# Two layers of a gated delta rule beside a linear recurrence: its gates computed per token in columns instead of per head in rows

## What is computed

```python
def l2norm(x):
    return x * lax.rsqrt(jnp.sum(x * x, axis=-1, keepdims=True) + L2_EPS)
...
    q = l2norm(qkv[..., :512].reshape(B, S, 4, 128))          # after conv and silu
    k = l2norm(qkv[..., 512:1024].reshape(B, S, 4, 128))
    beta = jax.nn.sigmoid(gb)
    g = -jnp.exp(gdn_a_log) * jax.nn.softplus(ga + gdn_dt_bias)   # (token, head)
...
    gc = jnp.cumsum(g, within a chunk of 64)
    decay = jnp.exp(jnp.where(tril, gc[..., :, None] - gc[..., None, :], -jnp.inf))
    a_mat = jnp.where(strict, (k * beta) @ k.T * decay, 0.0) + I
    u, w = solve(a_mat, [v * beta, k * beta * exp(gc)])
    # scan over chunks uses q * exp(gc), k * exp(gc_last - gc), exp(gc_last)
```

## Time and profile before

| | us |
|---|---|
| median of 3 runs (lowest, highest) | 2260.6 (2257.97, 2263.47) |
| the profiled execution, its own time | 2264.03 |
| its span | 2261.9 |
| PE busy in it | 2154.1 |
| DVE, ACT, POOL busy in it | 1321.4, 903.5, 622.4 |

### The profile page before, as it was taken

How to read it: one execution, slowest core, us unless ns; L and a number is a source line. 1 busy time by engine, 2 the same in 40 slices (tenths; PEclk the granted TensorE clock), 3 DMA queues, 4 the chain that set the end, 5 groups by cost and what they waited for, 6 DMA issues and landing times.

```text
span 2261.9 us, 25487 instructions
## 1 busy us (share of the span) xinstructions
PE 2154.1 (95%) x9704; PEld 1601.9 (71%) x9704; DVE 1321.4 (58%) x2006; ACT 903.5 (40%) x1410; POOL 622.4 (28%) x282
## 2 busy tenths in 40 slices
PE   8999999998999999999998999999999899999997
PEld 6777864766777864677766866777777578667776
DVE  4787845456788845457588724434165987244341
ACT  4432254433432354433563233445245543244441
POOL 2232420333233320333332300124433322002252
PEclk9999999997999999999998999999999899999999
DMA  6223321422323321323221012113232200111132
...
DMA packets 48047, 180.24 MB, mean 80 GB/s; under 512 B 5554, under 2 KB 6450, under 8 KB 46520
## 3 DMA queue, kind: packets, MB, share of 16 engines
...
...
q10 hardware_dynamic: 128, 0.13, 0.0%
...
## 4 chain that ended last, share of the span: by engine, by line
PE 72%; DVE 23%; ACT 2%; issue 2%; DMA 0%; DVEq 0%; ACTq 0%
PE bank L575 12%; PE bank L584 11%; PE bank L589 11%; PE bank L692 5%; PE bank L846 4%; PE bank L704 2%; PE bank L1058 2%; PE bank L1038 2%; PE bank L859 1%; PE bank L711 1%; PE bank L775 1%; PE bank L620 1%; PE bank L789 1%; DVE arena L1819 1%; DVE arena L1823 1%
## 5 line engine op out<-in xcount | busy, mean ns | idle before, releaser
L2344 POOL TENSOR_TENSOR w_lo<-wraw,w_hi 128x1024 fp32r<-128x1024 f32 (+1 forms) x222 | 548.6, 2473 | 1469.1 <-ACT w_hi L1126 1469.1
L1126 ACT ACTIVATE w_hi<-wraw 128x1024 fp32r<-128x1024 f32 (+1 forms) x222 | 233.7, 1053 | 679.7 <-PE bank L589 438.3
L575 PE MATMUL bank<-h_hi,w_hi 128*128 128x512 f32 (+1 forms) x1584 | 416.8, 406 | 8.7 <-ACT w_hi L1126 7.5
L584 PE MATMUL bank<-h_lo,w_hi 128*128 128x512 f32 (+1 forms) x1584 | 395.2, 391 | 0.2
L589 PE MATMUL bank<-h_hi,w_lo 128*128 128x512 f32 x1552 | 383.5, 389 | 0.0
L575 PEld LDWEIGHTS bank<-h_hi,w_hi 128*128 128x128 f32 (+1 forms) x1584 | 298.0, 191 | 107.9 <-issue 45.2
L584 PEld LDWEIGHTS bank<-h_lo,w_hi 128*128 128x128 f32 (+1 forms) x1584 | 298.4, 188 | 66.7 <-DVE h_lo L1658 1.7
L589 PEld LDWEIGHTS bank<-h_hi,w_lo 128*128 128x128 f32 x1552 | 290.1, 187 | 61.8
L692 PE MATMUL bank<-arena,wdir 128*128 128x512 f32 x256 | 114.3, 598 | 0.0
L846 PE MATMUL bank<-arena,wdir 128*128 128x512 f32 x208 | 97.8, 606 | 0.1
L2255 DVE TENSOR_TENSOR bank<-bank,con 128x128 f32<-128x128 f32 x64 | 19.2, 299 | 133.2 <-PE bank L1044 132.1
...
## 6 DMA issues: line engine op xcount, KB each, us to landing
...
```

What stands on the lines that cost most here:

```text
L575: mm(ps[0:wd, 0:S], hi[:, k, :].bitcast(F32R), h_hi[:, k, :].bitcast(F32R), start=k == 0 and not begun, stop=False)
L584: ins = mm(ps[0:wd, 0:S], hi[:, k, :].bitcast(F32R), h_lo[:, k, :].bitcast(F32R), start=False, stop=bool(parts) and k == KT - 1)
L1126: a(w_hi[:, n % 2, 0:f].bitcast(F32R), wraw[:, n % 2, 0:f], ACT.Copy).then_inc(hi_done, 1)
L2344: nc.gpsimd.tensor_tensor(w_lo[:, n % 2, 0:f].bitcast(F32R), wraw[:, n % 2, 0:f], w_hi[:, n % 2, 0:f], ALU.subtract).then_inc(lo_done, 1)
```

## The change

The gates are computed with tokens in the partitions: 128 partitions by 16 columns (4 blocks of 128 tokens, 4 heads) in place of 4 partitions by 512 tokens.

- `gba`'s 36 rows are copied as they are and turned by 4 transposes (`gT`). Sigmoid, the added bias, absolute value, exponential and `log1p_of` work on 128 x 16.
- The scan within a chunk becomes a product with the 0/1 matrix `incl`, and the chunk's total a product with a new matrix `chunk_` (`gC`, 2 matmuls). `constants` sends 128 more columns for it.
- Beta and cumulative decay are turned back as eight rows at once (`gR`, 4 transposes), split in two float32r parts by ACT (`rows_hi`) and DVE (`rows_lo`). `sel` shrinks to one column a row, read with stride 0.
- The 8 sums of squares become 32 products of a 128 x 128 block with one column of ones (`l2`), rooted and inverted as 128 x 32 and turned back by 4 transposes (`lR`). `l2sq` has room for all 8 squares.
- The 16 transposes `gN` and their copy go, since the columns are there already.
- The orders of PE, ACT and DVE are written anew around these.

The diff, cut to its core:

```diff
+        jobs += [("gc", l, j) for j in range(4, 8)] + [("gba", l), ("gc", l, 8), ("gc", l, 9), ("gT", l)]
+        jobs += [("gc", l, 10), ("gc", l, 11), ("lz", l, 0), ("gC", l), ("lz", l, 1), ("gR", l), ("lz", l, 2), ("lz", l, 3)]
+        jobs += [("gB", l, h, 1) for h in range(H)] + [("l2", l), ("mq", l, 0), ("lR", l), ("mq", l, 1)]
+        jobs += [("lb", l, j) for j in range(8)] + [("mq", l, 2)]
+        jobs += [("gB", l, h, 0) for h in range(H)] + [("mkv", l, j) for j in range(3)]
...
-                    return mm(ps[:, 0:S], sel[:, h * P:(h + 1) * P].bitcast(F32R), rows[:, n, :].bitcast(F32R),
+                    return mm(ps[:, 0:S], sel[:, h:h + 1].bitcast(F32R).broadcast_to([PAIR, P]), rows[:, n, :].bitcast(F32R),
...
+                ps = take("gT", l)
+                pe.wait_ge(*after("g_raw", l))
+                for tt in range(NT):
+                    ins = nc.tensor.transpose(ps[:, tt * GATES:(tt + 1) * GATES], graw[:, tt * P:(tt + 1) * P], ident[0:GATES, 0:GATES])
+                ins.then_inc(filled("gT", l), 1)
+                tile("gc", 10)
+                tile("gc", 11)
+                tile("lz", 0)
+                ps = take("gC", l)
+                pe.wait_ge(*after("g_col", l))
+                mm(ps[:, 0:16], incl, g_acc, start=True, stop=True)
+                mm(ps[:, 16:32], chunk_, g_acc, start=True, stop=True).then_inc(filled("gC", l), 1)
+                tile("lz", 1)
+
+                def to_rows(job, src):
+
+                    ps = take(*job)
+                    for tt in range(NT):
+                        ins = nc.tensor.transpose(ps[0:2 * H, tt * P:(tt + 1) * P], src(tt), ident)
+                    ins.then_inc(filled(*job), 1)
+
+                pe.wait_ge(*after("decays", l))
+                to_rows(("gR", l), lambda tt: gN[:, 16 * tt:16 * tt + 2 * H])
+                tile("lz", 2)
+                tile("lz", 3)
                 if l == 0:
                     pe.wait_ge(*after("sel"))
+                for h in range(H):
+                    ps = take("gB", l, h, 1)
+                    pe.wait_ge(*after("gc_rows", l))
+                    broadcast(ps, H + h, 1).then_inc(filled("gB", l, h, 1), 1)
+                ps = take("l2", l)
+                for n in range(8):
+                    pe.wait_ge(*after("l2_sq", l, n))
+                    for tt in range(NT):
+                        ins = mm(ps[:, 8 * tt + n:8 * tt + n + 1], l2sq[:, n, tt * P:(tt + 1) * P], ones[:, 0:1],
+                                 start=n == 0 and tt == 0, stop=n == 7 and tt == NT - 1)
+                ins.then_inc(filled("l2", l), 1)
+                tile("mq", 0)
+                pe.wait_ge(*after("l2_inv", l))
+                to_rows(("lR", l), lambda tt: l2col[:, 8 * tt:8 * tt + 8])
+                tile("mq", 1)
...
-                link(a(gates[:, 0, :], bank("gba", l)[0:H, 0:S], ACT.Sigmoid))
-                a(tmp4[:, 1, :], bank("gba", l)[32:32 + H, 0:S], ACT.Copy).then_inc(release("gba", l), 1)
-                for j in range(8, 12):
-                    conv_mid(j)
+                a(graw, bank("gba", l)[0:GATES, 0:S], ACT.Copy).then_inc(release("gba", l), 1)
+                act.wait_ge(*read("gba", l))
+                act.sem_inc(up("g_raw", l), 1)
+                conv_mid(8)
+                conv_mid(9)
+                act.wait_ge(*full("gT", l))
+                a(gcol4[:, :, 0, :], bank("gT", l)[:, 0:NT * GATES].rearrange("p (t r) -> p t r", t=NT)[:, :, 0:H],
+                  ACT.Sigmoid).then_inc(up("g_sig", l), 1)
+                conv_mid(10)
+                conv_mid(11)
 
                 act.wait_ge(*after("ga_dt", l))
-                link(a(tmp4[:, 1, :], tmp4[:, 0, :], ACT.Abs))
-                link(a(tmp4[:, 1, :], tmp4[:, 1, :], ACT.Exp, scale=-1.0))
-                a(small[0:H, 44:45], heads4[:, l, 0:1], ACT.Exp).then_inc(up("ga_y", l), 1)
+                link(a(g_y, g_x, ACT.Abs))
+                link(a(g_y, g_y, ACT.Exp, scale=-1.0))
+                a(g_scale, heads[:, l, 0, :], ACT.Exp).then_inc(up("ga_y", l), 1)
...
-                    if j == 3:
-                        act.wait_ge(*after("gc_sb", l, 3))
-                        for q in range(4):
+                    if j in (3, 7):
+                        act.wait_ge(*after("gc_sb", l, j))
+                        for q in range(j - 3, j + 1):
                             a(l2sq[:, q, :], gqkv(q), ACT.Square).then_inc(up("l2_sq", l, q), 1)
                     if j in (2, 9):
                         await_split("lz", l, 1 if j == 2 else 2)
+                    if j == 5:
+                        rows_hi(("gR", l), 1, 0)
                     if j in (5, 8):
                         silu_z(j // 4 - 1)
                 await_split("lz", l, 3)
-                act.wait_ge(*full("l2", l, 0))
-                act.wait_ge(*after("gc_sb", l, 7))
-                for j in range(4, 8):
-                    a(l2sq[:, j % 4, :], gqkv(j), ACT.Square).then_inc(up("l2_sq", l, j), 1)
-                row_root(("l2", l, 0), row_q, 1)
                 silu_z(2)
-                keep(("mq", l, 0), cq[:, 0, :])
                 silu_z(3)
-                row_root(("l2", l, 1), row_k, 1)
                 act.wait_ge(*after("decays", l))
-                a(tmp4[:, 0, :], gates[:, 1, :], ACT.Exp).then_inc(up("exp_gc", l), 1)
-                a(gates[:, 3, :], tmp4[:, 1, :], ACT.Exp).then_inc(up("exp_rest", l), 1)
-                keep(("mq", l, 1), cq[:, 1, :])
-                keep(("mq", l, 2), cq[:, 2, :])
-                act.wait_ge(*full("gN", l))
-                a(gN[:, :], bank("gN", l)[:, 0:64], ACT.Copy).then_inc(release("gN", l), 1)
...
+                act.wait_ge(*full("l2", l))
+                a(l2col, bank("l2", l)[:, 0:32], ACT.Sqrt, bias=EPS6).then_inc(release("l2", l), 1)
+                act.wait_ge(*read("l2", l))
+                act.sem_inc(up("l2_root", l), 1)
+                keep(("mq", l, 0), cq[:, 0, :])
+                rows_hi(("lR", l), 0, 1)
+                keep(("mq", l, 1), cq[:, 1, :])
+                keep(("mq", l, 2), cq[:, 2, :])
+                keep(("mkv", l, 0), ckv[:, 0, :])
...
+                dve.wait_ge(*after("g_sig", l))
+                raw = bank("gT", l)[:, 0:NT * GATES].rearrange("p (t r) -> p t r", t=NT)[:, :, 32:32 + H]
+                v.tensor_tensor(th(g_x), raw, heads[:, l, 1, :].unsqueeze(1).broadcast_to([P, NT, H]),
+                                ALU.add).then_inc(release("gT", l), 1)
+                dve.wait_ge(*read("gT", l))
+                v.sem_inc(up("ga_dt", l), 1)
+                conv(10)
+                conv(11)
+                dve.wait_ge(*after("ga_y", l))
+                log1p_of(g_y, g_s, g_s2, g_acc)
+                link(v.tensor_scalar(g_x, g_x, 0.0, None, ALU.max))
+                link(v.tensor_tensor(g_acc, g_acc, g_x, ALU.add))
+                v.scalar_tensor_tensor(th(g_acc), th(g_acc), -1.0, g_scale.unsqueeze(1).broadcast_to([P, NT, H]), ALU.mult,
+                                       ALU.mult).then_inc(up("g_col", l), 1)
...
-                log1p_of(tmp4[:, 1, :], gates[:, 1, :], gates[:, 2, :], gates[:, 3, :])
-                link(v.tensor_scalar(tmp4[:, 0, :], tmp4[:, 0, :], 0.0, None, ALU.max))
-                link(v.tensor_tensor(gates[:, 3, :], gates[:, 3, :], tmp4[:, 0, :], ALU.add))
-                link(v.tensor_scalar(gates[:, 3, :], gates[:, 3, :], small[0:H, 44:45], -1.0, ALU.mult, ALU.mult))
-                link(v.memset(tmp4[:, 1, :], 1.0))
-                link(v.memset(tmp4[:, 1, 0:S:CH], 0.0))
-                link(v.tensor_tensor_scan(gates[:, 1, :], tmp4[:, 1, :], gates[:, 3, :], 0.0, ALU.mult, ALU.add))
-                gc3 = gates[:, 1, :].rearrange("p (c i) -> p c i", i=CH)
-                v.tensor_tensor(tmp4[:, 1, :].rearrange("p (c i) -> p c i", i=CH), gc3[:, :, CH - 1:CH].broadcast_to([H, NC_, CH]), gc3, ALU.subtract).then_inc(up("decays", l), 1)
-                dve.wait_ge(*after("decays", l))
-                pair(2, gates[:, 1, :]).then_inc(up("gc_rows", l), 1)
-                for j in range(4):
+                def rows_lo(job, n, turn):
+
+                    dve.wait_ge(*after("row_hi", l, turn))
+                    v.tensor_tensor(rows[32:PAIR, n, :].bitcast(F32R), bank(*job)[0:2 * H, 0:S], rows[0:2 * H, n, :],
+                                    ALU.subtract).then_inc(release(*job), 1)
+                    dve.wait_ge(*read(*job))
+
+                dve.wait_ge(*full("gC", l))
+                tot = bank("gC", l)
+                link(v.tensor_copy(gcol4[:, :, 1, :], th(tot[:, 0:16])))
+                v.tensor_tensor(th(g_rest), th(tot[:, 16:32]), gcol4[:, :, 1, :], ALU.subtract).then_inc(release("gC", l), 1)
+                dve.wait_ge(*read("gC", l))
+                v.sem_inc(up("decays", l), 1)
+                for j in range(2):
                     dve.wait_ge(*read("lz", l, j))
```

(75 more changed lines are left out.)

61 lines of the change are left out of this document (27 added, 34 removed).

## The result

| | before | changed |
|---|---|---|
| median, us (lowest, highest, runs) | 2260.74 (2257.97, 2263.99, 8) | 2271.47 (2264.3, 2273.82, 8) |
| the profiled execution, own time, us | 2264.03 | 2270.88 |
| its span, mean granted clock | 2261.9, 0.967 | 2268.8, 0.962 |
| PE, DVE busy in it, us | 2154.1, 1321.4 | 2164.5, 1268.5 |

Ratio changed to before: 1.0040, 95% interval [1.0030, 1.0051]. The kernel is slower by 0.4%, some 9 us by the ratio. The forecast was 2262.8, within 2253 to 2273; its likeliest case was "no difference", at 0.47. The changed kernel lies inside the range, but the loss is clear of the scatter, and its time is that of rival 1 (2271). DVE lost 53 us of work, and PE works 10 us longer.

A forecast was written before the change was run, and what follows sets the result against it. PE bounds the kernel (busy 2154.1 of 2261.9 us), held by DVE in the stretch changed. First layer +0.7, second +1.5, start 0: +2.2 on 2260.6 gives 2262.8 us, 8 in 10 within 2253 to 2273.

The forecast's parts named there:

- rival 1: Clock low from `gR` over the sums to `mq` 1, PE's chain 17.5 against 15.3: +4.2 a layer, 2271; chance 0.27.
- no difference: Whole kernel: time within 0.2% of before (2256.1 to 2265.1 us); chance 0.47.
- `gC`'s wait: Before `gC`, behind `lz` 0: PE waits 2.8 us for DVE's small operations on the gates.
- The 18 small operations: DVE's gate arithmetic on 128 x 16 before `gC`: 3.8 us, none counted as caught by POOL.
- `decays`: Before `gR`: DVE reads them behind the recurrence, two operations lengthened by POOL, at 1161.6; PE waits 9.65 us.
- End of `lz` 3: Last tile behind `gR`: ends at 1175.4, with 2.1 us for low clock after the wait.
- The chain of ACT and DVE: From the end of `lz` 3 to `lR`, through differences, masks' exponentials, root and reciprocal: 15.3 us.
- PE's chain: From the end of `lz` 3 to `lR`: 1.16 + 5.6 (sums) + 5.44 (`mq` 0), 12.2 to 14.5 us.
- The second decides: At `lR`: the chain of ACT and DVE, 15.3 us, is longer than PE's and sets the start, 1190.7.
- Behind `lR`: From `lR` to the end of `mkv` 2: ends at 1222.7, with 0.7 us for low clock in `mq` 1.
- Rival 3: PE waits for the gates nowhere: 15.4 us a layer less, 2230; chance 0.04.
- slower: Whole kernel slower than before beyond 0.2%, from rival 1 and the forecast's upper part; chance 0.32.

The follow-up runs named there:

- e2: Changed kernel with DVE reading the chunk totals (`decays`) after the first of four parts of the recurrence: 2254.9 us, ratio to before 0.9969.
- e3: e2 with `gC` and `gR` each a tile later and the turned rows' split right behind the recurrence: 2250.0 us, ratio to before 0.9943.
- e6: Changed kernel with the 32 one-column products in two runs of 16, `mq` 0 between them: 2271.3 us, ratio to before 1.0037.
- e7: Changed kernel with squares and ones of the sums rounded to fp32r, one pass, two equal columns a product: 2260.6 us, ratio to before 0.9995.
- e10: e3 and e7 together, with the norms' root on ACT ahead of the masks' exponentials: 2232.9 us, ratio to before 0.9872.

## Why the prediction was right or wrong

By the times from the end of `gc` 9 the forecast can be laid against the trace step by step (forecast start 1126.65, measured 1124.77).

- **`gC`'s wait**, forecast 2.8: 2.75. The 18 small operations, 3.8: 3.8. Right. What I left out is the low clock behind it: `gC` and `lz` 1 took 3.6 us more than the 5.7 I had counted. It cost nothing there, since the wait for `decays` was shorter by nearly the same: 5.86 in place of 9.65. Without that cover (e2) it is on the path, and e3 takes 2.5 of it off.
- **`decays`** 34.95 us after the start: 34.85 (1159.62). The order of DVE and both collisions with POOL were right. None of the small operations was caught by POOL (0.17 to 0.25 each); two of the recurrence's were. The Trainium skill ("SBUF — State Buffer", on the shared port pair) calls the pair an exclusive lock; by that rule the two of 2.7 us are expected, and the trace agrees.
- **End of `lz` 3** 48.75 after the start: 48.9 (1173.65). Right, with its 2.1 for the clock.
- **The chain of ACT and DVE** from there, 15.3: 15.2 (1188.85). Right.
- **PE's chain, 12.2 to 14.5: 18.7.** This step failed, and with it "The second decides": "32 one-column products; 24 such took 3.52 us". The row's counts are instructions, and an fp32 product is two of them, as the changed kernel's 64 for 32 show: the row is of 12 products, not 24. Read rightly give 0.29 to 0.46 a product, 9.4 to 14.7 for 32, and with the 1.16 and 5.44 of the sum a chain of at least 16.0, over the 15.3 of ACT and DVE. The sums measured 10.34. At full clock throughout they would be an estimated 7.2 (twice e6's 3.6 for 16), so of the 4.7 us that the forecast of 5.6 lacked, some 1.6 is the count and 3.1 the clock that fell within them. `mq` 0 behind them lost another 2.0 by the clock (7.40 against 5.44); the forecast had up to 2.3 for that. "FP8 and Floating Point Precision" of the Trainium skill ("TensorE Precision Notes") gives true fp32 four passes through the array, which could have warned me; the rows show two instructions a product, and e7, with one, halves the sums.
- **Behind `lR`**, 32.0: 31.4, as `mq` 1 had its full clock (0.7 allowed).

In sum +3.5 at `lR` and -0.6 behind it, 2.9 us a layer, 5.8 in all: 2.2 forecast and 5.8 give 8.0. The forecast was counted to L2147; there the measured loss is 7.9, and by the ratio of the times some 9.

**Rival 1** named the time, its condition (PE's chain over 15.3) and a low clock in the sums; it had the price of the sums from the same misread row (7.4 at half clock, where 10.34 came at a mixed one), made up by a clock low from `gR` on. In the trace the clock was full again by 1166, fell in the sums, and was full in `mq` 1, where the rival had 2.0 for it. So it came true for half its reason, and that its 2271 is so close is partly luck: it had 4.2 us a layer over the forecast, and the trace shows 2.9. The Trainium skill's rule ("TensorE: Matmul & The Clock Gate", "What's actually happening"), read by busy share, would have made this rival fall away; the trace does not agree, with 0.50 while PE was busy 2.00 of 2.00. **Rival 3** (2230) was out of reach with this order of DVE, as the prediction said; e10 comes to 2233 by changing that order, the sums' passes and the place of the root.

Chances: "slower" had 0.32, "same" 0.47. With the row read rightly, rival 1's condition would have held by every figure in it, and "slower" should have had the larger chance.
